# New orders at both borders of gate and up, for the block sums in its loop, and for loads and row scaling in the down phase

## The reference

```python
# y: 1024 channels of two head groups, each RMS-normed (from a recurrence and a convolution)
x = x + jnp.einsum('bse,ed->bsd', y, w_out[l])
h = rmsnorm(x, norm_ffn[l])
f = jax.nn.silu(jnp.einsum('bsd,df->bsf', h, w_gate[l])) * jnp.einsum('bsd,df->bsf', h, w_up[l])
x = x + jnp.einsum('bsf,fd->bsd', f, w_down[l])
return rmsnorm(x, norm_final)
```

## Time and profile before

| | us |
|---|---|
| median of 3 runs | 2006.25 |
| lowest, highest | 2002.8, 2006.49 |
| the profiled execution | 2004.53 |
| its span, from first to last instruction | 2002.7 |
| around the span | 1.8 |
| mean granted clock of TensorE | 0.979 of full speed |

### The profile page before, as it was taken

One profiled execution on the slowest core, in us unless ns is written; L12 is line 12 of the kernel. 1 busy time (PEld: TensorE's weight loads), 2 busy tenths in 40 slices (PEclk: granted clock), 3 DMA queues, 4 the chain that ended last, 5 costly groups with the idle time before them and its releaser, 6 DMA issues.

```text
span 2002.7 us, 22412 instructions
## 1 busy us (share of the span) xinstructions
PE 1893.2 (95%) x8338; PEld 1554.0 (78%) x8338; DVE 1125.7 (56%) x1023; ACT 816.8 (41%) x936; POOL 1249.3 (62%) x490
## 2 busy tenths in 40 slices
PE   6999899978999799999999789999999899999997
PEld 5888687756888678878878668888888688888886
DVE  5899899988554635454454644444453123434446
ACT  6356856585553523333233433233333222322234
POOL 2477477964542567887666556766766666766663
PEclk9999999988999899999999989999999999999999
DMA  5223232245768334445234622233233565565555
GB/s 165 64 60 98 74 95 74 77 144 182 241 207 280 101 100 131 140 136 152 84 100 129 219 87 86 93 115 101 89 112 134 220 248 205 175 217 180 180 189 209
DMA packets 242335, 284.97 MB, mean 142 GB/s; under 512 B 12078, under 2 KB 167726, under 8 KB 241754
## 3 DMA queue, kind: packets, MB, share of 16 engines
q1 hardware_dynamic: 242266, 284.04, 42.9%
HBM read 201.68 MB, written 82.31 MB: 142 GB/s over the span
## 4 chain that ended last, share of the span: by engine, by line
PE 69%; POOL 12%; issue 7%; DVE 5%; DMA 3%; ACT 2%; SPq 1%; POOLq 0%; DVEq 0%; ACTq 0%
PE ps L1828 17%; PE ps L1829 17%; PE ps L1830 17%; PE acc L1828 6%; PE acc L1829 5%; PE acc L1830 5%; POOL b_lo L826 2%; POOL t_lo L832 2%; POOL gt L872 1%; POOL quad L881 1%; DVE acc L1597 1%; POOL fs L890 1%; DMA y_raw<-d_scr 1%; POOL f_lo L917 1%; DMA wd_raw<-in_w_down 1%
## 5 line engine op out<-in xcount | busy, mean ns | idle before, releaser
L1597 DVE SCALAR_TENSOR_TENSOR acc<-glu,par,acc 128x1024 f32<-128x1024 f32 x232 | 298.9, 1288 | 7.2
L832 POOL TENSOR_TENSOR t_lo<-t_sum,t_hi 128x2048 fp32r<-128x2048 f32 x44 | 205.0, 4658 | 135.2 <-ACT t_hi L1241 135.2
L826 POOL TENSOR_TENSOR b_lo<-m_raw,b_hi 128x1536 fp32r<-128x1536 f32 x44 | 163.9, 3724 | 164.5 <-ACT b_hi L1236 164.5
L917 POOL TENSOR_TENSOR f_lo<-f_raw,f_hi 128x2048 fp32r<-128x2048 f32 (+1 forms) x42 | 180.9, 4306 | 133.2 <-ACT f_hi L1381 133.2
L1636 DVE TENSOR_TENSOR t_sum<-m_raw 128x512 f32<-128x512 f32 x88 | 131.1, 1491 | 214.0 <-PE ps L1830 97.1
L1828 PE MATMUL ps<-h_hi,w_hi 128*128 128x512 f32 x512 | 201.9, 394 | 4.6 <-POOL w_lo L720 2.7
L1829 PE MATMUL ps<-h_lo,w_hi 128*128 128x512 f32 x512 | 200.0, 391 | 0.0
L1830 PE MATMUL ps<-h_hi,w_lo 128*128 128x512 f32 x512 | 200.0, 391 | 0.0
L1828 PE MATMUL ps<-wd_hi,f_hi 128*128 128x512 f32 x462 | 181.4, 393 | 9.9 <-POOL wd_lo L924 9.9
L1381 ACT CAST f_hi<-f_raw 128x2048 fp32r<-128x2048 f32 (+1 forms) x42 | 74.2, 1768 | 274.6 <-PE ps L1830 178.2
L1829 PE MATMUL ps<-wd_lo,f_hi 128*128 128x512 f32 x462 | 181.0, 392 | 0.0
(11 more groups left out here) (212 smaller groups left out, 4603.0 us busy)
## 6 DMA issues: line engine op xcount, KB each, us to landing
f_raw<-f_scr SPq DMA_DIRECT2D x35, 1024.0 KB, 5.0
wd_raw<-in_w_down SPq DMA_DIRECT2D x60, 512.0 KB, 6.6
f_scr<-fs SPq DMA_DIRECT2D x110, 256.0 KB, 2.0
m_raw<-in_w_gate SPq DMA_DIRECT2D x88, 256.0 KB, 4.0
m_raw<-in_w_up SPq DMA_DIRECT2D x88, 256.0 KB, 5.0
w_raw<-in_w_in SPq DMA_DIRECT2D x32, 512.0 KB, 5.3
f_scr<-gt SPq DMA_DIRECT2D x44, 256.0 KB, 2.0
xt<-in_x SPq DMA_DIRECT2D x16, 512.0 KB, 3.7
```

What stands on the lines that cost most here:

```text
L826: g.tensor_tensor(b_lo[b][:, :, :, :], m_raw[b][:, 0:3], f32(b_hi[b][:, :, :, :]), ALU.subtract).then_inc(s_mlo, 1)
L832: g.tensor_tensor(t_lo[b][:, :, :, :], t_sum[b][:, :, :, :], f32(t_hi[b][:, :, :, :]), ALU.subtract).then_inc(s_mlo, 1)
L917: g.tensor_tensor(f_lo[j % 3][:, 0:n], f_raw[j % 2][:, 0:n], f32(f_hi[j % 3][:, 0:n]), ALU.subtract).then_inc(s_dlo, 1)
L1597: ins = v.scalar_tensor_tensor(out=into[:, :], in0=t[:, k:k + HALF], scalar=col(j, R_DW + k), in1=acc[:, :], op0=ALU.mult, op1=ALU.add)
```

## The change

- **POOL, first border:** row 15's `y_lo_part` goes ahead of `raw_lo(0, 0)` and `a_low(0)`; `a_low(6)` goes between `raw_lo` and `sums_lo` of matrix 1.
- **POOL, loop:** `quad_sums(k)` is cut into two parts of two sums. Part 0 comes in `gate_block` ahead of `sums_lo`, part 1 in `up_block` behind the first `hidden`. SP's loads and stores of quads keep their places.
- **ACT:** at both borders the casts of operands 3 to 6 come earlier, `raw_hi` of the first up matrix too.
- **DVE, first border:** scaling of row 14 moves from its own turn to behind the weight sums of matrix 0; `a_low` of operand 3 goes ahead of the scaling of row 15.
- **DVE, loop:** in gate blocks (b = 0) the first `weight_sum` goes from ahead of `hidden21`, `f_sum6` and `sum11` to behind them. In the second half's first block the `a_low` go ahead of the weight sums, and operand 3 goes into the block before.
- **SP, border between the halves:** operand 3's store comes after the load of operand 4, operand 4's store after all seven loads.
- **SP, down phase:** loads of steps 2 and 3 go ahead of stores; x2 rows are loaded at other steps.
- **DVE, last pass:** rows 4 and 5 are scaled after `wd_sum` of step 41, with rows 6 and 7.

```diff
@@ SP, last step of the first half
-                        if n in (2, 5):
-                            store_operand({2: 3, 5: 4}[n], h, FI - 1, FI - 1)
-                    store_f(h, FI - 1, FI - 1, (1, 5, 6))
+                        if n == 4:
+                            store_operand(3, h, FI - 1, FI - 1)
+                    store_f(h, FI - 1, FI - 1, (4, 1, 5, 6))
@@ def load_step(j)
-                    sp_.wait_ge(s_fst[m - 1], 16 * (NH * FI - (j < 2)))
+                    sp_.wait_ge(s_fst[m - 1], 16 * (NH * FI - (j < 3)))
@@ SP, start of the down phase
             load_step(0)
             load_step(1)
+            load_step(2)
             store_f(1, FI - 1, FI - 1, (3, 4, 1, 5))
+            load_step(3)
             sp_.wait_ge(s_pr[6], MATS)
             sp_.wait_ge(s_f21, NH * FI)
+            for e in (0, 1):
+                load_x2(row_tile(e, 0))
             store_f(1, FI - 1, FI - 1, (6, 7, 2))
...
-            for j in range(2, len(STEPS)):
+            for j in range(4, len(STEPS)):
                 load_step(j)
-                for e in {2: (0, 1), 3: (2, 3), 4: (4, 5), 5: (6, 7)}.get(j, ()):
+                for e in {4: (2, 3, 4), 5: (5, 6, 7)}.get(j, ()):
                     load_x2(row_tile(e, 0))
@@ POOL, rows
             for w in range(3, NT):
+                y_lo_part(w)
                 if w == NT - 1:
                     raw_lo(0, 0)
                     pool.wait_ge(s_sum0, 4)
                     a_low(0)
-                y_lo_part(w)
@@ POOL, loop
-            def quad_sums(k):
+            def quad_sums(k, part):
                 pool.wait_ge(s_qld, 64 * (k + 1))
...
+                    if n // 2 != part:
+                        continue
...
-            def gate_block(m, i=None, first=False):
+            def gate_block(m, i=None, first=False, k=None):
                 raw_lo(m + 1, 1)
                 if i is not None:
                     f_sum(2, i - 1, first)
+                if k is not None:
+                    quad_sums(k, 0)
                 sums_lo(m + 1, 1)
...
                 hidden(m, i, 0)
+                if k is not None:
+                    quad_sums(k, 1)
                 if not last:
                     sums_lo(m + 1, 0)
...
-                    gate_block(first + 2 * i, FI * h + i if i else None, i == 1)
-                    if h == 0 and i == 0:
+                    k = QUADS.index(i) if i in QUADS else None
+                    if i == 0:
+                        raw_lo(1, 1)
                         a_low(6)
-                    up_block(first + 2 * i + 1, FI * h + i, first=h == 0 and i == 0)
-                    if i in QUADS:
-                        quad_sums(QUADS.index(i))
+                        sums_lo(1, 1)
+                    else:
+                        gate_block(first + 2 * i, FI * h + i, i == 1, k)
+                    up_block(first + 2 * i + 1, FI * h + i, first=h == 0 and i == 0, k=k)
@@ ACT, both borders
                     sums_hi(0, 0)
+                    a_high(3)
                     row_std(w)
...
-            a_high(3)
... in gate_block
                 if starts == 0:
-                    a_high(4)
+                    a_high(5)
                     h2_copy(NT - 2)
+                    raw_hi(m + 1, 1, i + 1)
                 if starts == 1:
-                    second_a_high(3)
-                    second_a_high(4)
+                    second_a_high(5)
+                    raw_hi(m + 1, 1, i + 1)
                 if starts is None:
                     raw_hi(m + 1, 1, i + 1)
                 copy_p5(m, i, 0, first)
+                if starts == 0:
+                    a_high(6)
                 silu(i, 0)
-                if starts == 0:
-                    a_high(5)
-                if starts == 1:
-                    second_a_high(5)
                 copy_u2(m, i, 0, first)
                 if starts == 0:
                     h2_copy(NT - 1)
-                    a_high(6)
-                if starts is not None:
-                    raw_hi(m + 1, 1, i + 1)
+                if starts == 1:
+                    second_a_high(6)
                 sums_hi(m + 1, 1)
                 silu(i, 1)
                 silu(i, 2)
-                if starts == 1:
-                    second_a_high(6)
... in up_block
                     sums_hi(m + 1, 0)
+                    if ends == 0:
+                        second_a_high(3)
                     copy_y(m + 1, i + 1, 0)
+                    if ends == 0:
+                        second_a_high(4)
...
+            a_high(4)
             copy_y(0, 0, 0, first=True)
@@ DVE, rows: row_scaled(w) is what L1649 to L1657 did
             def first_weight_sums():
                 for n in range(4):
                     weight_sum(0, 0, n, 1)
+                row_scaled(NT - 2)
+                a_low(0, 2)
...
                 if w == NT - 1:
-                    a_low(0, 2)
+                    a_low(0, 3)
+                if w != NT - 2:
+                    row_scaled(w)
@@ DVE, def matrix_block
-                    if not last:
+                    if not last and b:
                         weight_sum(m + 1, 1 - b, 0, count)
                     if not b:
                         hidden21(i - 1)
                         f_sum6(i - 1, second)
                     sum11(m, i, b, first)
+                    for n in early if not b else ():
+                        a_low(1, n)
                     if not last:
-                        for n in range(1, 4):
-                            weight_sum(m + 1, 1 - b, n)
-                    for n in early:
+                        for n in range(1 if b else 0, 4):
+                            weight_sum(m + 1, 1 - b, n, count)
+                    for n in early if b else ():
                         a_low(1, n)
                     if not b and not early:
                         f_sum2(i - 1, second)
                 sum12(m, i, b, first)
+                for n in between:
+                    a_low(1, n)
...
-            a_low(0, 3)
...
-                    matrix_block(MH, FI, 0, count=FI + 1, early=(3, 4, 5), late=(6,))
+                    matrix_block(MH, FI, 0, count=FI + 1, early=(4, 5), between=(6,))
...
-                             early=(0, 1) if h + 1 < NH else (), late=(2,) if h + 1 < NH else ())
+                             early=(0, 1) if h + 1 < NH else (), late=(2, 3) if h + 1 < NH else ())
@@ DVE, last pass
-                if p == 6 and k < 4:
-                    for e in range(2):
-                        final_row(2 * k + e, 1)
+                if p == 6:
+                    for e in {0: (0, 1), 1: (2, 3), 3: (4, 5, 6, 7)}.get(k, ()):
+                        final_row(e, 1)
```

More of the change, by code:

```diff
@@ L895, in gate_block, with up_block @@
                     f_sum(2, i - 1, first)
+                if k is not None:
+                    quad_sums(k, 0)
                 sums_lo(m + 1, 1)
-            def up_block(m, i, last=False, first=False):
+            def up_block(m, i, last=False, first=False, k=None):
                 if not last:
@@ L1640, in first_weight_sums, with row_scaled @@
                     weight_sum(0, 0, n, 1)
-            for w in range(NT):
-                if w:
-                    add_row(w, first_weight_sums if w == NT - 1 else None)
-                if w == 0:
-                    norm_scale(1)
-                if w == NT - 1:
-                    a_low(0, 2)
+                row_scaled(NT - 2)
+                a_low(0, 2)
+            def row_scaled(w):
                 dve.wait_ge(s_std2, w + 1)
@@ L1657, in _ @@
                                        in1=g_row[:, :], op0=ALU.mult, op1=ALU.mult).then_inc(s_hn, 1)
+            for w in range(NT):
+                if w:
+                    add_row(w, first_weight_sums if w == NT - 1 else None)
+                if w == 0:
+                    norm_scale(1)
+                if w == NT - 1:
+                    a_low(0, 3)
+                if w != NT - 2:
+                    row_scaled(w)
                 for m, first in NORM_STEP.items():
@@ L1717, in f_sum2, with matrix_block @@
                 v.tensor_tensor(fs[:, 4], gt[:, 0, TILE:HALF], gt[:, 1, TILE:HALF], ALU.add).then_inc(s_fsd, 1)
-            def matrix_block(m, i, b, first=False, count=None, last=False, early=(), late=(), second=False):
+            def matrix_block(m, i, b, first=False, count=None, last=False, early=(), between=(), late=(), second=False):
                 if first and not b:
```

## The result

The changed kernel takes 2030.93 us (median of 4 runs, 2027.37 to 2032.8), the kernel before in the same comparison 2004.53 (4 runs, 2001.82 to 2006.49): ratio **1.0126**, 95% interval 1.0112 to 1.0141. It is 1.3% slower. Forecast were 2036, within 2016 to 2056.

The account below looks back on a forecast made before the run. TensorE (PE), busy 1893.2 of 2002.7 us, was taken as the bound: its matmuls plus waits. Terms summed to +30.3 on 2004.5, giving 2034.8; with the median 1.7 higher the forecast was 2036 us, range 2016 to 2056.

Parts of the forecast that it names:

- Block sums, +60: Loop steps 1 to 4: POOL waits for each quad's load with t_lo queued behind, so PE stops four times; +60 us.
- A + 21.9: Landing of quad k = 0, 21.9 us after A, the moment PE ends product 6 of matrix 2i-1.
- A + 28.7: Landing of quads k = 1 to 3, 28.7 us after PE ends product 6 of matrix 2i-1.
- Steps 1 to 5, -3.1: Gate and up loop: quad_sums no longer stands between f_sum and b_lo; 3.1 us less.
- Steps 6 to 9, -4.2: Gate and up loop: DVE's sum11 now comes ahead of the first weight sum; 4.2 us less.
- First border, -8: Row 15, products of matrix 0: y_lo ready in time, product 6 starts earlier; 8 us less, bounds -2 and -13.
- Border between the halves, -4.7: Matrix 22 between the gate and up halves: product 6 starts earlier; 4.7 us less, bounds 0 and -12.
- Start of down, -7.7: Start of down phase: third and fourth loads go earlier, two waits for wd_lo vanish; 7.7 us less, bounds -4 and -8.
- End of down, -2: Last wd_lo: rows 4 and 5 now follow the last wd_sum; 2 us less, bounds +1 and -6.
- the quad is there in time: Rival for the loop: quads land by A + 14.6, only the gains stay, 1975 us; chance 0.06.
- Short chain: Rival for the loop: wait for the previous quad's store gone or hidden, +44 instead of +60, 2020 us; chance 0.10.
- The borders give nothing: Rival: gains at both gate and up borders and the end are eaten; 2050, up to 2066 us; chance 0.13.

Follow-up runs that it names:

- early quads: Changed kernel, but SP loads each quad one step ahead and stores it in the step in which it is summed: 1968.78 us, ratio 0.9838.
- sums at the end: Changed kernel with all four block sums of a quad back at the end of the step, everything else kept: 1971.41 us, ratio 0.9841.
- `f_sum2` first: The early quads kernel with f_sum2 ahead of a_lo of operand 6 in the second half's first block: 1963.39 us, ratio 0.9809.
- sums one place later: Changed kernel with the first two block sums behind sums_lo instead of ahead, SP's order as in the change: 1995.99 us, ratio 0.9969.

## Why the prediction was right

Right in sign, in mechanism and, within 0.3%, in size. No step failed outright. That it came so near is in part luck: errors inside the largest term cancel, the borders gave more than their terms, and the term for the end of the down phase can't be confirmed.

- **Block sums, +60.** The four steps are 60.3 us too long. Forecast were landings at A + 21.9 and A + 28.7; POOL's first sums start 22.8 us after step 1 begins and 27.7 after step 2 does (746.51 - 723.68, 801.02 - 773.32). Stops were forecast at 8.6 and three times 14.1, they were 9.1 and 13.1 to 13.7; the clock was put at 2.3 each (its rows, ten matmuls in 4.4 us instead of 2.3, give only 2.1) and took 2.8. So the standing was put 1.7 us too high and the clock 1.9 too low, and 60 against 60.3 is nearer than the parts deserve. Taking the block sums back (57 us by the ratios) or putting them in alone (56.6) shows that the cause is this edit, and the early quads show that it is the landing and not the sums.
- **Steps 1 to 5, -3.1.** Shown by the early quads (190.6 us, 193.4 with the sums at the end of the step) and by the same split in the kernel before (2.9 us at the median, 190.5 us against 193.9).
- **Steps 6 to 9, -4.2.** They take 974.41 to 1126.57 in the changed kernel, 152.2; alone the edit gave 4.4 us.
- **First border, -8.** Alone 10.6, within the bounds of -2 and -13. The stops for `hn` (2.06 and 0.45 us) and for `t_lo` (2.86) came as laid out. The 2.6 us above the term are about what the interval leaves open (8.0 to 13.4 us). The term ends at the start of product 6 and leaves out the clock behind it: from there to step 1 the kernel before needs 24.8 us (708.29 to 733.08), the first 4 of them at PEclk 0.50, the changed kernel 22.2 us (701.52 to 723.68) at 1.00. Not every profile has this gain: with the first border alone it is 24.3 us.
- **Border between the halves, -4.7.** Alone 7.4 (by the interval 4.6 to 10.2, so 4.7 is just inside). The two stops of 5.50 us are the ones that were named as late next, `sum11` behind POOL's chain, and `sum22` behind `f_sum2`. The chain also had `f_sum2` end 5.3 us after `a_lo(6)`, behind POOL's `t_lo`; in the trace these 5.0 us are the length of `f_sum2` itself, since the profile counts its standing as busy. With this border alone the chain ends about 1.7 us sooner than laid out (its step 10 begins 0.8 us later than in the kernel before, and `sum22` starts at 1151.74 where 1152.6 was laid out), and the stretch from product 6 to the next `hidden21` is 0.75 us shorter.
- **Start of down, -7.7.** Alone 8.0. The third load is issued at 1592.02, ahead of the stores, and PE no longer waits there. The last `hidden21` of the loop comes 35.4 us later than before (1598.64 against 1563.26), so this is the 1556.6 of the forecast.
- **End of down, -2.** This term is not borne out in the changed kernel's own profile. PE waits 4.29 us for the last `wd_lo`, 4.01 before. `wd_sum` did get free, 1.23 us instead of 5.62, but the scalings behind it took its place:

```profile
1989.52 1.23 DVE L1801 TENSOR_TENSOR wd_raw<-wd_raw 128x1024 f32<-128x1024 f32 x1 [8.75 <-DMA wd_raw<-in_w_down]
...
1992.24 5.43 DVE L1823 SCALAR_TENSOR_TENSOR x<-x,rstd,gfin 128x1024 f32<-128x1024 f32 x1
```

```profile
1991.51 5.08 POOL L927 TENSOR_TENSOR f_lo<-f_raw,f_hi 128x2048 fp32r<-128x2048 f32 x1 [3.06 <-ACT f_hi L1393]
1996.55 3.32 POOL L934 TENSOR_TENSOR wd_lo<-wd_raw,wd_hi 128x1024 fp32r<-128x1024 f32 x1
```

DVE and POOL take turns, and POOL loses 1.4 us of what it needs. But five more profiles have the same code at this place, and there the wait is 3.8 us (sums at the end), 3.1 (`f_sum2` first), 2.0 and 1.8 (early quads, twice) and 1.8 (sums one place later), so up to the 2 us that were forecast; it is 4.0 in all kernels without the edit. This is the profile of the early quads:

```profile
PE ps L1851 <- POOL wd_lo L935: 1.8, 1, 1.8
```

```profile
1924.02 2.10 DVE L1802 TENSOR_TENSOR wd_raw<-wd_raw 128x1024 f32<-128x1024 f32 x1 [6.67 <-DMA wd_raw<-in_w_down]
```

In all six `wd_sum` starts when its load has landed, and the wait falls in the order in which that is ahead of PE's arrival: 6.2 us ahead in the changed kernel, then 6.7, 7.7, 8.1, 8.3 and 8.6. So behind row scaling, which was moved, stood the landing of the last `wd_raw`, which the term did not have. Why it lands sooner in some kernels is open, and the sign of the term in the time too; where scaling also waits for `wd_lo` the wait is 1.3 us.

The sum of the terms was +30.3, the spans differ by 28.3, the medians by 26.4. The single parts at the two borders gained 5.3 us more than their terms. All five parts together come to +26.2 us (56.6 - 4.4 - 7.4 - 10.6 - 8.0). Of the 5.1 us that the forecast is too high, 3.9 are the terms and 1.2 its starting point, 2005.7 us, where the median of before in the comparison is 2004.53.

Of the rivals, *the quad is there in time* is the version with early quads: 1968.78 us, forecast at 1975. It was refused for the right reason, since SP's order was not changed. *Short chain* would have had four stops of 9; only the first is so. *The borders give nothing* is ruled out by the three parts run alone.

The estimate by the Trainium skill ("SBUF — State Buffer", "Summary: rules for kernel authors"), 2.9 us for a quad, is again not what the trace shows: 5.6 us from 795.43 to POOL's first sum. Its sum, 2025, is no nearer to 2030.93 than 2036 is, and the stops speak against it: 13.1 to 13.7 us is not 11.

## What to carry to other kernels

An operation that is put ahead of another in a queue brings its own wait with it. Before moving one, read when its data land by the queue of the engine that issues the load, and compare this with the moment at which the work behind it is needed. Here moving the sums in POOL's order cost 57 us and the same move was worth 3 once the loads were issued a step earlier. Second, a price for a late operation must go on through what is queued behind it and through the clock; the variant that put the sums one place later had waits of 3.5 to 4.5 us for `b_lo`, and each such step cost 7.4 to 8.8.

## What the runs showed of the hardware that was not expected

- **DVE and POOL exclude each other for whole instructions, and who comes first decides the price.** DVE's `f_sum2` takes 0.68 us alone and 5.00 behind POOL's `t_lo`, which had begun 0.7 us before it. When DVE's `a_lo` is first, `t_lo` takes 5.83 us instead of 4.6, longer by about the 1.4 us that `a_lo` still had to run. The Trainium skill ("SBUF — State Buffer", "Who interferes with whom") says that a DVE instruction with two SBUF inputs contends with a GpSimd instruction that reads SBUF, that the shared ports are an exclusive lock, and that the order of issue decides which of the two is blocked. The rows agree. Here, putting the short `f_sum2` ahead of the other engine's long `t_lo` gained 4.0 us.
- **A short stop can cost as much clock as a long one.** After 3.52 us of standing, PE ran at 1.2 GHz for 6.1 us, which cost 3.05 us. The four stops of 9.1 to 13.7 us cost 2.8 each. Length alone does not set the price: after a stop of 4.51 us in the same kernel the low clock lasted 3.4 us, and behind stops of 2.06, 2.86 and 2.61 us at the first border of the changed kernel PEclk stayed at 1.00, while the same 2.61 us in the kernel with `f_sum2` first were followed by 0.50.
